# The second layer's input units: half of each step's loads issued from ScalarE's queue instead of SP's

## What is computed

```python
def spatial_gating_layer(x, norm_g, w_in, v_norm_g, w_s, b_s, w_out):
    h = rms_norm(x, norm_g)
    u, v, z = jnp.split(h @ w_in, 3, axis=-1)          # w_in: 2048 x 12288
    ...
    y = u * mixed * jax.nn.silu(z)
    return y @ w_out

def forgetting_attention_layer(x, norm_g, w_in, f_bias, q_norm_g, k_norm_g, w_out):
    h = rms_norm(x, norm_g)
    proj = h @ w_in                                    # w_in: 2048 x 8208
    q, k, v, z, f_logit = jnp.split(proj, [...], axis=-1)
    ...
    return y @ w_out
```

## Time and profile before

| | |
|---|---|
| median of three runs | 2382.68 us (2379.84 to 2383.91) |
| the profiled execution, its own time | 2386.65 us |
| its span | 2384.8 us |
| TensorE matmuls busy | 2291.4 us, 96% |
| VectorE busy | 1617.2 us, 68% |
| ScalarE busy | 1065.6 us, 45% |
| SP's DMA queue (q1) | 366.53 MB, 54.7% of 16 engines' span |
| ScalarE's DMA queue (q10) | 41.98 MB, 4.7% |
| GpSimd's DMA queue (q0) | 67.28 MB, 8.1% |

### The profile page before, as it was taken

The page is one execution under the profiler, slowest core; times in us unless marked ns, Lnnn a source line. Parts: engine busy times, 40 slices in busy tenths (PEclk is TensorE's granted clock), DMA queues, the critical chain, the costliest instruction groups (busy, mean ns, idle before and its releaser), DMA issues.

```text
span 2384.8 us, 26500 instructions
## 1 busy us (share of the span) xinstructions
PE 2291.4 (96%) x10413; PEld 1866.3 (78%) x10413; DVE 1617.2 (68%) x1676; ACT 1065.6 (45%) x1319; POOL 135.3 (6%) x185
## 2 busy tenths in 40 slices
PE   7999999999999999999999989999979999999999
PEld 5777788788887878878888877777767777778887
DVE  7778777877877777753222577776766877666665
ACT  5755545454544445452223444444443444344332
POOL 0011011000000000000000000100100000111000
PEclk9999999999999999999999999999999999999999
DMA  6678777776777677675344478885698897845333
GB/s 235 228 251 269 238 248 247 227 235 217 236 227 227 221 229 236 210 250 145 97 114 114 114 172 167 206 264 158 200 235 179 194 281 236 287 137 164 104 96 115
DMA packets 232892, 477.48 MB, mean 200 GB/s; under 512 B 19680, under 2 KB 26384, under 8 KB 231744
## 3 DMA queue, kind: packets, MB, share of 16 engines
q1 hardware_dynamic: 191056, 366.53, 54.7%
q0 software_dynamic: 18576, 67.28, 8.1%
q10 hardware_dynamic: 23136, 41.98, 4.7%
HBM read 393.90 MB, written 81.82 MB: 199 GB/s over the span
## 4 chain that ended last, share of the span: by engine, by line
PE 73%; DVE 10%; DMA 8%; issue 6%; ACT 1%; POOL 0%; SPq 0%; DVEq 0%; ACTq 0%; POOLq 0%
PE ps L1204 15%; PE ps L1206 15%; PE ps L1205 15%; PE ps L1362 5%; PE ps L1361 5%; PE ps L1363 5%; DVE u_lo L1651 4%; DMA t_rows<-t 4%; DMA raw<-in_b_w_in_dram 3%; PE ps L1584 2%; PE ps L1586 2%; PE ps L1585 2%; DVE raw L1636 2%; DMA raw<-t_rows 2%; PE ps L1507 2%
## 5 line engine op out<-in xcount | busy, mean ns | idle before, releaser
L719 ACT ACTIVATE u_hi<-raw 128x1536 fp32r<-128x1536 f32 (+1 forms) x320 | 544.7, 1702 | 820.0 <-PE ps L1206 783.2
L1651 DVE TENSOR_TENSOR u_lo<-raw,u_hi 128x1536 fp32r<-128x1536 f32 (+1 forms) x320 | 647.0, 2022 | 237.0 <-ACT u_hi L719 236.2
L1204 PE MATMUL ps<-u_hi,x1h 128*128 128x512 f32 x1280 | 514.5, 402 | 61.6 <-DVE u_lo L1651 55.4
L1205 PE MATMUL ps<-u_lo,x1h 128*128 128x512 f32 x1280 | 505.4, 395 | 0.0
L1206 PE MATMUL ps<-u_hi,x1l 128*128 128x512 f32 x1280 | 504.5, 394 | 0.0
L1204 PE MATMUL ps<-u_hi,x2h 128*128 128x512 f32 x960 | 381.7, 398 | 5.6 <-DVE u_lo L1651 4.9
L1206 PE MATMUL ps<-u_hi,x2l 128*128 128x512 f32 x960 | 375.6, 391 | 0.0
L1205 PE MATMUL ps<-u_lo,x2h 128*128 128x512 f32 x960 | 375.4, 391 | 0.0
L1204 PEld LDWEIGHTS ps<-u_hi,x1h 128*128 128x128 f32 x1280 | 244.1, 191 | 143.5 <-DVE u_lo L1651 79.3
L1206 PEld LDWEIGHTS ps<-u_hi,x1l 128*128 128x128 f32 x1280 | 244.1, 191 | 52.8
L1205 PEld LDWEIGHTS ps<-u_lo,x1h 128*128 128x128 f32 x1280 | 243.9, 191 | 48.2
(11 more groups left out here) (232 smaller groups left out, 2420.3 us busy)
## 6 DMA issues: line engine op xcount, KB each, us to landing
raw<-in_a_w_in_dram SPq DMA_DIRECT2D x280, 512.0 KB, 4.4
raw<-in_b_w_in_dram SPq DMA_DIRECT2D x184, 512.0 KB, 5.5
t_rows<-t ACTq DMA_DIRECT2D x160, 256.0 KB, 5.0
raw<-t_rows SPq DMA_DIRECT2D x160, 256.0 KB, 5.0
w_raw<-in_a_w_out_dram SPq DMA_DIRECT2D x128, 256.0 KB, 2.9
w_raw<-in_b_w_out_dram SPq DMA_DIRECT2D x64, 256.0 KB, 2.7
vz<-vz_rows POOLq DMA_DIRECT2D x16, 512.0 KB, 5.5
t<-yT_rows SPq DMA_DIRECT2D x28, 256.0 KB, 3.5
```

The costliest lines, as they stand in the source:

```text
L719: act.activation(u_hi[:, u_of(g), 0:n, :], raw_of(g)[:, 0:n, :], ACT.Copy).then_inc(hi1_ready, 1)
L1204: pe.matmul(dst[:, t, :], a, u_hi[:, s, pos, :], start=first, stop=False, skip_group_check=more)
L1205: pe.matmul(dst[:, t, :], a, u_lo[:, s, pos, :], start=False, stop=False, skip_group_check=more)
L1651: dve.tensor_tensor(u_lo[:, u_of(g), 0:n, :], raw_of(g)[:, 0:n, :], u_hi[:, u_of(g), 0:n, :].bitcast(F32), ALU.subtract).then_inc(lo1_read ...
```

## The change

From the fourth step of the second layer on (`by_act`: g >= STEPS + 3), SP issues the first load of a step only. The second one (rows 2k+1 in phase 0, the stored t2 in phase 1) is issued by ScalarE, in a new function `load_part` that runs right after the hi split of step g-2. It waits for the same lo split as SP's load does, and in phase 1 for the store of t2 as SP did. The function `weights` moves out of SP's block and stays as it was. 125 loads move: 61 of 512 KB and 64 of 256 KB. Nothing is computed in another way.

```diff
+        def by_act(g):
+            return g >= STEPS + 3
...
                 if ph == 0:
                     sp.dma_start(slot[:, 1:3, :], k1).then_inc(loaded, 16)
+                    if by_act(g):
+                        return
                     if first(u):
                         sp.dma_start(slot[:, 0, :], k2[:, 0, :]).then_inc(loaded, 16)
                     else:
@@
                     q = u * KP + k
                     sp.dma_start(slot[:, 0:4:3, :], k2).then_inc(loaded, 16)
+                    if by_act(g):
+                        return
                     sp.wait_ge(t2_stored[q % 2], (q // 2 + 1) * 16)
                     sp.dma_start(slot[:, 2, :], t2_dram[k, :, :]).then_inc(loaded, 16)
@@ high(u, ph, k), on ScalarE
                 act.activation(u_hi[:, u_of(g), 0:n, :], raw_of(g)[:, 0:n, :], ACT.Copy).then_inc(hi1_ready, 1)
+                if by_act(g + 2) and g + 2 < STEPS + NB_U * 2 * KP:
+                    load_part(g + 2)
+
+            def load_part(g):
+                u, ph, k = g // (2 * KP), g // KP % 2, g % KP
+                slot, loaded, q = raw_of(g), raw_wait(g)[0], u * KP + k
+                act.wait_ge(lo1_ready, g - 2)
+                if ph == 0:
+                    k2 = weights(u, (2 * k + 1) * P)
+                    if first(u):
+                        act.dma_start(slot[:, 0, :], k2[:, 0, :]).then_inc(loaded, 16)
+                    else:
+                        act.dma_start(slot[:, 0:4:3, :], k2).then_inc(loaded, 16)
+                else:
+                    act.wait_ge(t2_stored[q % 2], (q // 2 + 1) * 16)
+                    act.dma_start(slot[:, 2, :], t2_dram[k, :, :]).then_inc(loaded, 16)
```

More of the change, by code:

```diff
@@ L418, in y_of, with weights @@
             return y_s[:, s, :, :] if s < 3 else y_s3[:, :, :]
+        def weights(u, row):
+            if u < VU:
+                return a_v[row:row + P, u, :, :]
+            if u < NU:
+                return a_uz[row:row + P, :, (u - VU) * FB:(u - VU + 1) * FB]
+            c = GROUP[u - UB] * FB
+            return (b_qk if KIND[u - UB] == "qk" else b_vz)[row:row + P, :, c:c + FB]
+        def by_act(g):
+            return g >= STEPS + 3
         @block.sync
@@ L429, in load_x @@
                 sp.dma_start(stage[:, n % 3, :, :], x_t[:, :, c * 2 * P:(c + 1) * 2 * P]).then_inc(x_loaded[n % 3], 16)
[L431 to L437, removed]
             def load_step(u, ph, k):
```

## The result

| | before | changed |
|---|---|---|
| median, us | 2383.3 (2379.84 to 2384.51, 4 runs) | 2399.28 (2396.95 to 2402.1, 4 runs) |
| profiled execution: time, span, us | 2386.65, 2384.8 | 2396.95, 2395.1 |

The ratio is 1.007, with a 95% interval of 1.0053 to 1.0087: the change costs about 16 us. The two spans differ by 10.3 us only: the profiled execution of before, 2386.65, is above all four runs of its kernel, and that of the change is the earliest of its four. The mean granted clocks of the two are 0.990 and 0.994.

A forecast was written before the change was run, and what follows sets the result against it. It took TensorE, busy 96% of the span, as the bound, so only its idle time could change. Terms of +5.6, +1.4, +2.1 and -1.3 summed to +7.8 us on 2382.7, giving 2390.5 us, range 2370 to 2406.

The forecast's parts named there:

- The sign against it: Slow wide windows moving clearly more than 205 GB/s would show the forecast wrong.
- The quick one at 1653 has an engine share of 0.75: 0: Quick wide stretch at 1653: engines not full, so the later store of t2 costs 0.
- 0.7 us for each of the other three quick stretches: Quick wide stretches at 1553, 1926 and 2003: one t2 sum too late in each, +2.1 us together.
- 8 slow steps x 0.7 us: Slow stretches at 1462 and 1838: four steps each with a reduction behind the late store, +5.6 us.
- The loop over two steps: Wide steps: issue, 9.0 us to landing, VectorE's work, next issue but one; 12.5 us becomes 14.4, 7.2 a step.
- 1740: +1.4: Slow stretch at 1740: two steps with a gate product in the reduction's place, 2 x 0.7 us.
- The premise on queues: All DMA: one queue's transfers move in order and queues share the engines, so the store lands last, 9.0 us after issue.
- The end of the last unit: At 2050 to 2066, two load queues against GpSimd's one shorten TensorE's 4.07 us wait for the logits: -1.3 us.
- Issue times and ScalarE's own time: Second loads' shifted issue, at most 0.8 us, is covered; ScalarE's 125 more issues hide behind hi splits: both cost 0.
- Faster: Rival, 2370 us, chance 0.25: reads in two queues pass each other, so slow sets land sooner; 12 us less.
- No change: Rival, 2382 us, chance 0.29: both halves share the same engines and the store is no later than the weights.
- Much slower: Rival, 2402 us, chance 0.13: store behind everything in all wide steps, ScalarE's new wait holding up squares; bound +21.

The follow-up runs named there:

- e1: Changed kernel, with ScalarE's second load of each step issued after the store of t2, not ahead of it; 2375.84 us, ratio 0.9959 to the kernel before.
- e7: Changed kernel, with VectorE's t2 sum moved down to directly ahead of the lo split; 2384.06 us, ratio 0.9988 to the kernel before.
- e6: Kernel before, with SP issuing the second layer's stores of t2 behind both loads of a set; 2401.47 us, ratio 1.0069.
- e9: Kernel before, with SP issuing the second layer's stores of t2 between the two loads of a set; 2379.91 us, ratio 0.9977.
- e11: Kernel before, with the store of t2 still on ScalarE's queue but issued only after SP's whole set; 2400.4 us, ratio 1.0076.
- e10: Kernel before, with SP issuing the second layer's stores of t2 ahead of both loads of a set; 2377.79 us, ratio 0.9973.
- e8: Changed kernel, with the store of t2 issued before ScalarE's load and VectorE's t2 sum directly ahead of the lo split; 2384.07 us, ratio 0.9992.
- e2: Changed kernel, with ScalarE issuing the second load only in narrow steps (stored sums), SP keeping the second row in wide ones; 2382.47 us, ratio 0.9992.
- e3: Changed kernel, with ScalarE issuing the second load only in wide steps (second row), SP keeping the stored sums; 2404.14 us, ratio 1.0078.
- e4: Changed kernel, with the second layer's stores of t2 issued by SP behind its own row; 2398.03 us, ratio 1.0055.
- e5: Changed kernel, with the store of t2 issued before ScalarE's load and ScalarE loading in wide steps only; 2377.16 us, ratio 0.9964.

## Why the prediction was right or wrong

**Direction and mechanism: right.** It named the store of t2 as what gets worse and gave slower its largest chance. Of its signs these came: waits for the store over 50 us (70.6), more TensorE waits for u_lo (+16.2, against "8 or so"; the stretches at 1462 and 1838 have 8.4 of them, about half), nothing clear lost in the narrow phases (+0.7), and stores of t2 landing over 7 us after issue in slow steps. Line 749 in 1837 to 1870, against the earlier trace rows:

```profile
DMA to landing us min/median/max: 8.1/8.6/9.7
```

The second rows were to land no sooner than 8.5 us after issue; they took 8.0 to 9.5, with a median of 8.3, a little less. The sign against it, windows moving clearly more than 205 GB/s, didn't come (184). e1 shows the cause by swapping two issues, e7 by taking away what stands behind the wait.

**Size: half.** It put +7.8 us; about 16 were measured, inside the range given. Three steps carry the difference.

1. *"The quick one at 1653 has an engine share of 0.75: 0"* and 0.7 us for each of the other three quick stretches. This is the term that failed. The four quick stretches cost 1.9 + 3.5 + 3.5 + 1.8 = 10.7 us against 2.1. I had the store land late only where the engines are full. In the changed kernel it lands 5.3 to 6.5 us after issue in the stretch at 1653, 0.6 to 0.7 us behind the row issued 0.4 to 0.5 us before it. In the same stretch of the kernel before it lands 2.1 and 2.3 us after issue in the two steps where it goes ahead of the set, and 5.3 and 5.6 us in the two of the table above where it goes behind. The stretch at 1553 has one more thing in it: TensorE waits 3.45 us at once there (until 1580.84), and the first six matmuls behind it start some 0.43 us apart, later ones 0.23: by my estimate 1.2 of the 3.5 us. The granted clock in 1578 to 1586 is 0.79 and 0.78; the kernel before has 1.00 in that whole stretch. The 2 us a stretch that stood as the upper bound of a quick stretch would have been nearer, though two of the four went beyond it.
2. *8 slow steps x 0.7 us.* The 0.7 is the loop's 7.2 less the 6.5 of the trace; loop against loop it is 14.4 less 12.5 over two steps, 0.95 a step, which would have made +7.6. The stretches at 1462 and 1838 came to +7.9 against +5.6: 1838 to twice its term (5.4, not 2.8), 1462 to its own (2.6). TensorE's waits in 1447 to 1516 and in 1832 to 1891, where they were 5.1 and 7.6 (1832 to 1880):

```profile
PE ps L1229 <- DVE u_lo L1676: 8.7, 5, 3.0
...
PE ps L1229 <- DVE u_lo L1676: 12.4, 8, 2.4
```

   The loop over two steps leaves out GpSimd's part of a head's norm, which takes up the reduction's result. VectorE's waits for it went from 2.5 us to 7.5 (line 1978); they are 7.3 in e6, where the store is late too, and 2.8 in e1, but 5.1 in e9, which is quick. What they cost TensorE was not taken apart.
3. *1740: +1.4.* It fell by 3.0 us in the profile. It is the stretch that varies most: 58.5 in e1, 60.2 in e11, 56.4 in e10. Its granted clock varies with it, 0.92 before, 0.94 changed and in e1, 0.97 in e10, but TensorE's busy time there is only 0.6 us less in the changed kernel; the rest of the 3.0 is shorter waits. What moved them stays open.

**The premise on queues was half true.** I took it that one queue's transfers move in order and that queues share the engines, so that a store with ScalarE's queue to itself is early. e11 shows that a queue of its own doesn't make it early. For the changed kernel both readings give the same, since the store was behind loads in its queue and in SP's. But the second reading, that the order of issue across the queues decides, would have told me that before itself pays for late stores, and that the cure needs no second queue. The 8.3 in the earlier trace rows stood before me as the maximum of a group whose median I used.

The Trainium skill bears on it: DMA: Bandwidth & Descriptors, section Queues, rings and completion order, says that each engine goes round robin between its queues packet by packet. By that alone I would expect e11's store ahead of the weights, and it came in behind them. The same section says that the mark of completion is written only after every earlier write of that engine, across queues; e11's landing agrees in kind. No run here tells whether the store's data or only its mark is late.

**The end of the last unit** was put at -1.3 us, and the wait for nmin fell from 4.07 to 2.2, by 1.9. The wait is 2.0 to 2.5 in e1, e7 and e8 too, where ScalarE issues both kinds of load and the store. It is 3.8 in e2 and 4.0 in e3, where only one kind moved, 4.0 in e4, whose store is SP's, and 4.9 in e10, with one queue. Why it takes all three no run tells. What the wait costs is more than its length: right behind the 4.07 us TensorE ran at half its clock (0.50, the 1.2 GHz level), and in the changed kernel, behind 2.24 us, it ran at full clock. Windows of 3 us behind the wait, before and changed:

```profile
2069.00:2072.00 3.00, 2.51 (x6) 1.86 (x7) 1.82 (x7) 2.53 (x7) 0.00 (x0) 0.50 0.75 184
2072.00:2075.00 3.00, 3.00 (x9) 2.32 (x8) 2.33 (x4) 0.83 (x2) 0.00 (x0) 0.50 1.03 365
```
```profile
2082.00:2085.00 3.00, 3.00 (x15) 2.44 (x13) 2.06 (x2) 1.59 (x3) 0.00 (x0) 1.00 1.05 375
```

That is a cost my sums didn't have. The length of the last wait doesn't settle it alone: behind one of 2.00 us, at 1497.44, the kernel before fell to 0.50 as well, in 1499 to 1502. How much of the 3.2 us it makes is open: e2 falls to 0.50 at the same place and is itself 2.4 us shorter there than the kernel before.

**Issue times and ScalarE's own time**, put at 0: e2 bears the first out for narrow steps. In wide steps e1 and e5, with 125 and 61 more issues on ScalarE, lose nothing against the kernel before, so neither term can be large.

**Rivals.** *Faster*, by reads of two queues passing each other, falls. The windows of the changed kernel:

```profile
1454.00:1462.00 8.00, 7.17 (x32) 5.63 (x31) 4.03 (x3) 3.83 (x2) 0.00 (x0) 1.00 0.99 161
1838.00:1878.00 40.00, 31.47 (x131) 23.77 (x131) 29.48 (x23) 16.82 (x14) 0.00 (x0) 1.00 0.95 184
```

At 1454 full engines move 161 GB/s, before 157; at 1838 184, before 205. At 1454 e3 and e5, where two queues read as well, have 150 and 157. *No change* falls by the interval. *Much slower*, 2402, lies 3 us above the median and e3 reached it, but its mechanism, ScalarE's new wait holding up the squares, isn't what the traces show: the store's place alone makes the loss in e6, where ScalarE has no such wait. The upper bound's other half, the store behind everything in quick wide steps too, is nearest to what happened.

Does a second queue give anything once the store is early? e1 (0.9959, up to 0.9974) against e10 (0.9973, from 0.996): the intervals overlap. A difference of 3 us is not resolved.

## What to carry to other kernels

In this kernel a small transfer that something waits for soon had to be issued ahead of the large ones whose landing has slack, whichever queue each was in: look at the order of issue across all queues, not within one. When a load moves to an engine that also issues a store, ask whose wait the store ends and what stands behind that wait on the waiting engine; here the swap of two neighbouring issues was worth 23 us between medians, and moving the load to another queue nothing that could be measured. And read the maximum of a group of landings, not the median: a group with 3.3 and 8.3 in it can have two causes. Last, compare the granted clocks of two traces before reading a difference of a few us between them.

## What the runs showed of the hardware that I had not expected

- A 256 KB store, alone in ScalarE's queue, landed 3.3 us after issue when it was issued 0.77 us ahead of a set of 1 MB in SP's queue, and 7.8 to 8.3 us after issue when it was issued 0.12 to 0.73 us behind it. Issued between the two rows of a set, at 1469.44, it landed with the first.
- In e4 the order of issue did not decide alone: a store 0.4 us behind a 512 KB row of its own queue landed 2.2 us after that row, when a second row had been issued in the other queue 0.9 us after the store. That both share the engines from then on would explain it; no run here separates that.
- Two queues of slow reads moved about what one did: 161, 157 and 150 GB/s in the changed kernel, e5 and e3, with the engines 0.99 to 1.00 busy, where one queue moved 157.
- A wait of TensorE can be paid twice: behind 4.07 us of idle time its granted clock was 0.50 in 2069 to 2075, behind 3.45 us six matmuls ran at half pace. Behind 2.24 us it stayed at 1.00, and behind 2.00 us elsewhere it fell to 0.50 for 3 us, so more than the one wait decides.
